# Adding the bias of the gates on TensorE and taking tanh straight from PSUM, in a two-block transformer kernel

## The reference, cut to what matters

```
mod = silu(c) @ w_ada + b_ada
u = modulate(rmsnorm(h, norm_mix_g), sh1, sc1)
z = u @ w_in
...
ga, gb = split(sigmoid(u @ w_gate + b_gate), 2)
h = h + g1 * ((ga * y_ret + gb * y_dsa) @ w_o)
```

## Time and profile before

| what | us |
|---|---|
| median of 3 runs (lowest, highest) | 908.58 (907.78, 908.63) |
| the profiled execution | 907.57 |
| its span in the trace | 905.9 |
| PE busy in the span | 891.5 |
| DVE, ACT, POOL busy | 680.6, 548.2, 209.8 |

### The profile page before, as it was taken

How to read it: one execution, slowest core, us unless ns; L and a number is a source line. 1 busy time by engine, 2 the same in 40 slices (tenths; PEclk the granted TensorE clock), 3 DMA queues, 4 the chain that set the end, 5 groups by cost and what they waited for, 6 DMA issues and landing times.

```text
span 905.9 us, 12878 instructions
## 1 busy us (share of the span) xinstructions
PE 891.5 (98%) x4423; PEld 733.7 (81%) x4423; DVE 680.6 (75%) x961; ACT 548.2 (61%) x885; POOL 209.8 (23%) x218
## 2 busy tenths in 40 slices
PE   8999999999999999999999999999999999999996
PEld 6888877888887888888867889778788888888885
DVE  5867688765767578778686544699899897968984
ACT  6656776788557443443485446754775585656763
POOL 4696037545312011111005500014300000000001
PEclk9999999999999999999999999999999999999998
DMA  8656756666865899999646657634374098969941
GB/s 283 189 172 205 223 160 197 222 190 229 275 190 181 308 296 314 320 304 312 209 126 202 188 155 241 208 102 155 117 250 152 6 344 302 321 238 337 377 166 47
DMA packets 124007, 199.59 MB, mean 220 GB/s; under 512 B 9601, under 2 KB 73793, under 8 KB 123697
## 3 DMA queue, kind: packets, MB, share of 16 engines
q1 hardware_dynamic: 118048, 177.17, 59.6%
q0 software_dynamic: 5904, 21.71, 7.4%
HBM read 197.79 MB, written 2.62 MB: 221 GB/s over the span
## 4 chain that ended last, share of the span: by engine, by line
PE 86%; DVE 8%; issue 2%; DMA 1%; ACT 1%; POOL 1%; SPq 0%; ACTq 0%; DVEq 0%; POOLq 0%
PE lin L2926 21%; PE lin L2928 20%; PE lin L2927 20%; PE turn L3145 3%; PE sco L2928 2%; PE sco L2927 2%; PE sco L2926 2%; DVE w_lo L1913 2%; PE lin L3038 1%; PE lin L3039 1%; PE lin L3029 1%; DMA raw<-in_w_in_dram 1%; PE turn L3193 1%; PE sco L3266 1%; PE lin L3707 1%
## 5 line engine op out<-in xcount | busy, mean ns | idle before, releaser
L1913 DVE TENSOR_TENSOR w_lo<-raw,w_hi 128x1024 fp32r<-128x1024 f32 x220 | 288.3, 1323 | 104.6 <-ACT w_hi L1163 102.0
L1163 ACT ACTIVATE w_hi<-raw 128x1024 fp32r<-128x1024 f32 x220 | 229.1, 1059 | 104.5 <-PE lin L2928 84.0
L2926 PE MATMUL lin<-w_hi,a_hi 128*128 128x512 f32 (+2 forms) x600 | 237.2, 395 | 0.7 <-DVE w_lo L1913 0.5
L2928 PE MATMUL lin<-w_hi,a_lo 128*128 128x512 f32 (+2 forms) x600 | 230.6, 384 | 0.0
L2927 PE MATMUL lin<-w_lo,a_hi 128*128 128x512 f32 (+2 forms) x584 | 224.0, 384 | 0.0
L2926 PEld LDWEIGHTS lin<-w_hi,a_hi 128*128 128x128 f32 x600 | 112.8, 188 | 27.4 <-issue 4.5
L2928 PEld LDWEIGHTS lin<-w_hi,a_lo 128*128 128x128 f32 x600 | 112.8, 188 | 23.1
L2927 PEld LDWEIGHTS lin<-w_lo,a_hi 128*128 128x128 f32 x584 | 110.0, 188 | 19.9
L1127 POOL TENSOR_TENSOR arena<-x,rows 128x256 f32<-128x256 f32 x3 | 2.2, 744 | 195.3 <-DVE x L2904 195.3
L1069 POOL DMA_DIRECT2D arena<-in_w_ada_dram x32 | 17.0, 530 | 122.0 <-DVE mod L2016 121.5
L1041 POOL TENSOR_TENSOR mod<-mod,rows 128x1024 f32<-128x1024 f32 x16 | 38.1, 2382 | 24.9 <-ACT rows L1456 24.5
(11 more groups left out here) (572 smaller groups left out, 1886.3 us busy)
## 6 DMA issues: line engine op xcount, KB each, us to landing
raw<-in_w_in_dram SPq DMA_DIRECT2D x76, 512.0 KB, 4.1
arena<-in_w_ada_dram POOLq DMA_DIRECT2D x32, 512.0 KB, 5.6
raw<-in_w_ffn_gate_dram SPq DMA_DIRECT2D x22, 512.0 KB, 5.2
raw<-in_w_ffn_up_dram SPq DMA_DIRECT2D x22, 512.0 KB, 5.8
raw<-in_w_ffn_down_dram SPq DMA_DIRECT2D x22, 512.0 KB, 4.3
rows<-in_w_ada_dram SPq DMA_DIRECT2D x16, 512.0 KB, 4.2
raw<-in_w_o_dram SPq DMA_DIRECT2D x16, 512.0 KB, 4.7
raw<-in_w_gate_dram SPq DMA_DIRECT2D x16, 512.0 KB, 4.6
```

Of the source, the lines that this page charges most:

```text
L1163: act.activation(w_hi[:, s, :], raw[:, s, :], ACT.Copy).then_inc(hi_ready, 1)
L1913: dve.tensor_tensor(w_lo[:, s, :], raw[:, s, :], w_hi[:, s, :].bitcast(F32), ALU.subtract)\
L2926: pe.matmul(dst, l_hi, r_hi, start=start, stop=False)
L2928: return pe.matmul(dst, l_lo, r_hi, start=False, stop=stop)
```

## The change

The bias goes to PE. ACT rounds the bias (all 2048 columns on all partitions) into a high part `bias_hi`, in the space of `gate2`. DVE makes `bias_parts`, in place of the bias: partition 1 gets (high part minus bias), and all other partitions get minus the bias, rounded. DVE also makes a column `minus_r` that is -1 on partitions 0 and 1 and 0 elsewhere. PE begins each gate block with one product of this column, repeated over 128 columns, and 512 columns of `bias_parts`, for each half of the tokens; it leaves high part plus low part of the bias in the bank, and the products of the block add to that. The first of them waits for `bias_split`. ACT takes tanh from PSUM with the evacuation, two instructions of 128 by 512 for a block, one unit after the block ends. At the start, the gains are loaded and transposed first, and the second run of idle products has six in place of eight.

```
-    order += [(f"gt{n}", DK, "dve") for n in range(4)]
+    order += [(f"gt{n}", DK, "act") for n in range(4)]
...
+        minus_r = sb("minus_r", [P, 1], F32R)
...
+        bias_raw = rows[:, 2:4, :].rearrange("p a n -> p (a n)")
+        bias_parts = rows_r[:, 2:4, :].rearrange("p a n -> p (a n)")
...
+        bias_hi = arena_r[:, bt2:bt2 + 2 * D]
...
             sp.dma_start(cst[:, 0:P], consts[:, 0:P]).then_inc(ident_in, 16)
-            sp.dma_start(x[:, 0, :], ins["x"][0, 0:P, :]).then_inc(x_in[0], 16)
             sp.dma_start(rows[0:DK, 0, 0:P], ins["ln_mix_pre"].rearrange("a (k p) -> (a k) p", p=P))\
               .then_inc(rows_in[0], 16)
+            sp.dma_start(x[:, 0, :], ins["x"][0, 0:P, :]).then_inc(x_in[0], 16)
...
-            sp.wait_ge(evac["dve"], BLOCKS["gt3"][4])
+            sp.wait_ge(evac["act"], BLOCKS["gt3"][4])
...                                                         (ACT, fill)
-                        if BLOCKS[name][1] + BLOCKS[name][2] == unit_at[0]:
-                            if BLOCKS[name][3] == "act":
-                                evacuate(name)
-                        if name in ("gt0", "gt1", "gt2") and sum(BLOCKS[name][1:3]) + 2 == unit_at[0]:
-                            gate_tanh(name)
+                        late = 1 if name[:2] == "gt" else 0
+                        if BLOCKS[name][1] + BLOCKS[name][2] + late == unit_at[0] and BLOCKS[name][3] == "act":
+                            evacuate(name)
...                                                         (ACT, evacuate)
+                    if kind == "gt":
+                        i = act.activation(gate2[:, t, n * W:(n + 1) * W], lin[:, bank + t, :], ACT.Tanh, scale=0.5)
...                                                         (ACT, before fill(0, "jn7"))
+            act.wait_ge(rows_in[2], 48)
+            act.activation(bias_hi, bias_raw, ACT.Copy).then_inc(bias_high, 1)
             fill(0, "jn7")
...                                                         (ACT, DSA)
-                if i == 4:
-                    gate_tanh("gt3")
...                                                         (DVE, evacuate)
-                if kind == "gt":
-                    dve.wait_ge(rows_in[2], 48)
-                    bias = rows[:, 2 + n // 2, (n % 2) * W:(n % 2) * W + W]
-                    for t in range(NT):
-                        i = dve.tensor_tensor(gate2[:, t, c], lin[:, bank + t, :], bias, ALU.add)
-                    i.then_inc(done, 1)
...
-                        dve.wait_ge(tanh_ready, NT + 4)
+                        dve.wait_ge(evac["act"], BLOCKS["gt3"][4])
...                                                         (DVE, after fill(0, "jn7"))
+            dve.wait_ge(bias_high, 1)
+            dve.scalar_tensor_tensor(out=minus_r[:, :], in0=ident[:, 0:1], scalar=-1.0, in1=ident[:, 1:2],
+                                     op0=ALU.mult, op1=ALU.subtract)
+            dve.scalar_tensor_tensor(out=bias_parts, in0=bias_hi.bitcast(F32), scalar=ident[:, 1:2], in1=bias_raw, op0=ALU.mult, op1=ALU.subtract).then_inc(bias_split, 1)
             fill(1)
...                                                         (DVE, DSA)
-                if i == 3:
-                    evacuate("gt3")
...                                                         (PE, product_unit)
+                    if start and name[:2] == "gt":
+                        pe.wait_ge(bias_split, 1)
+                        n, start = int(name[2:]), False
+                        for t in tokens:
+                            pe.matmul(lin[:, 2 * (number % 2) + t, :], minus_r[:, :].broadcast_to([P, P]),
+                                      bias_parts[:, n * W:(n + 1) * W], start=True, stop=False)
...                                                         (PE, start)
             pe.wait_ge(ident_in, 16)
+            pe.wait_ge(rows_in[0], 16)
+            pe.transpose(sco[:, 0, 0:DK], rows[0:DK, 0, 0:P], ident[0:DK, 0:DK]).then_inc(gain_turned, 1)
             keep_clock(4)
             pe.wait_ge(x_in[0], 16)
             turn_all("x1.0", [col(x[:, 0, :], k) for k in range(4)])
-            pe.wait_ge(rows_in[0], 16)
-            pe.transpose(sco[:, 0, 0:DK], rows[0:DK, 0, 0:P], ident[0:DK, 0:DK]).then_inc(gain_turned, 1)
             turn_all("x1.1", [col(x[:, 0, :], k) for k in range(4, 8)])
-            keep_clock(8)
+            keep_clock(6)
```

More of the change, by code:

```diff
@@ L585, in two_blocks @@
         shift_out = sem("shift_and_scale_copied")
+        bias_high = sem("gates_bias_high_part_ready")
+        bias_split = sem("gates_bias_parts_ready")
         early_summed = sem("early_rows_summed")
@@ L1227, in evacuate @@
                 for t in range(NT):
-                    if kind == "in" and n >= 8:
+                    if kind == "gt":
+                        i = act.activation(gate2[:, t, n * W:(n + 1) * W], lin[:, bank + t, :], ACT.Tanh, scale=0.5)
+                    elif kind == "in" and n >= 8:
                         c = (n - 8) * W
@@ L1245, in evacuate @@
                 i.then_inc(evac["act"], 1)
[L1247 to L1252, removed]
             def block_loop(first, pairs, target, scale=lambda t: 1.0, start=None):
@@ L1945, in evacuate @@
                 done = evac["dve"]
-                if kind == "gt":
-                    dve.wait_ge(rows_in[2], 48)
-                    bias = rows[:, 2 + n // 2, (n % 2) * W:(n % 2) * W + W]
-                    for t in range(NT):
-                        i = dve.tensor_tensor(gate2[:, t, c], lin[:, bank + t, :], bias, ALU.add)
-                    i.then_inc(done, 1)
-                elif kind in ("pa", "ro"):
+                if kind in ("pa", "ro"):
                     gate = gate1 if kind == "pa" else gate2
                     if kind == "ro":
-                        dve.wait_ge(tanh_ready, NT + 4)
+                        dve.wait_ge(evac["act"], BLOCKS["gt3"][4])
                     for t in range(NT):
```

## The result

The changed kernel takes 915.28 us (median of 6 runs, 914.97 to 915.56) against 908.16 (6 runs, 907.51 to 908.63): a ratio of 1.0078, with an interval of 1.0066 to 1.0090. It is 7.1 us slower. The forecast was 914.6 with a range of 913.2 to 917.2. The profiled execution took 915.27 us with a span of 913.6, 7.7 above that of before.

A forecast was written before the change was run, and what follows sets the result against it. The prediction took PE, busy 891.5 of 905.9 us, to bound the kernel. It summed 4.65 + 1.84 - 0.59 + 0.1 = +6.0 us onto the median 908.58, giving 914.6 us, range 913.2 to 917.2.

The forecast's parts named there:

- low clock: PE behind the stall: the sum kept the high clock, or took its loss as under 1 us.
- sparse stage: Last two additions, for gt3, taken from DVE: PE has 0.1 us left to win there, left at nothing.
- rival A: PE's idle time in the stall drops its clock, costing 1 to 2.1 us more; 916.2 us, chance 0.36.
- stall: PE's first gate product waits for `bias_split` behind in-order work on ACT and DVE: 4.65 us, between 4.2 and 5.1.
- eight products: Bias products added on PE in the four gate blocks, 0.23 us each: +1.84 us.
- end of retention: PE's wait before the transposes at 635.70 goes, as DVE's chain shortens or PE comes later: -0.59 us.
- start: Gains loaded first, two idle products fewer on PE: +0.1 us, between -0.3 and +0.6.
- half of the slow stretch at the start: Upper price of a clock fall: 4.1 us at slow pace, as at the kernel's start, loses 2.1 us.
- two-pass bound: Eight broadcast products on PE priced like the float32 one, two passes and 0.95 us each: 7.6 us.
- two reasons: Before 635.70: DVE's chain 2.5 us shorter, or PE 1.4 us later by six products; either exceeds 0.59.
- B: Bias parts ready before PE's first gate product at 569.95, so no stall: +1.35 us, 909.9 us, chance 0.04.
- C: DVE sets the beat from 570 to 635, PE's hidden waits swallow the stall: -3.6 us, 905.0 us, chance 0.03.

The follow-up runs named there:

- e1: The changed kernel with ACT's rounding of the bias and DVE's making of the parts moved earlier, to idle places; 908.31 us, ratio 1.0003 to the kernel before.
- e5: The changed kernel with 18 idle products of 128 by 128 on PE just before its wait for the parts; 912.83 us, ratio 1.0053 to the kernel before.
- e2: The changed kernel without the eight bias products and PE's wait, the bias left out of the gates; 906.36 us, ratio 0.9983 to the kernel before.
- e7: e1 with two additions of 128 by 512 given back to DVE in the sparse stage, results unread; 909.02 us, ratio 1.0012 to the kernel before.
- e3: The kernel before with only the start's edits (gains loaded and transposed first, six idle products in place of eight); 907.63 us, ratio 0.9993.
- e8: The kernel before with the change for gt3 alone, its 512 columns of bias split early, the old start kept; 907.67 us, ratio 0.9992.
- e9: e8 with the edits of the start added; 906.83 us against 908.05 for the kernel before, ratio 0.9987.
- e10_few_idle_products: The changed kernel with 8 idle products of 128 by 128 on PE before its wait for the parts; 912.86 us, ratio 1.0055 to the kernel before.

## Why the prediction was right

The direction, the place and the largest term were right, and the total was 1.1 us too low (+6.0 forecast, +7.1 measured), as two terms that it had left out of the sum, the low clock and the sparse stage, go opposite ways. That the sum came as near as it did is in part luck: one omission of 2.0 us was offset by one of 0.8, and the median of three runs that it was added to, 908.58, was 0.4 above that of six. The measured time lies between the forecast and rival A's 916.2, and it was A's mechanism that happened. Point by point, from starts on PE in the two traces (the column makes 7.6, the spans differ by 7.7):

| term | forecast | trace | by experiment |
|---|---|---|---|
| stall | 4.65 | 4.68 | 7.0 with the clock (e1) |
| low clock | 0 (rival A: 1 to 2.1) | 2.0 | 2.4 (e5) |
| eight products | 1.84 | 1.84 | 1.95 (e1 less e2) |
| end of retention | -0.59 | -0.5 | |
| sparse stage | 0 | -0.8 | 0.7 (e7 less e1) |
| start | +0.1 | +0.4 (spread of executions) | -0.5, not clear of 0 (e3) |

**The stall.** PE came 0.40 us later to the transposes before it (570.00 against 569.60), so the stall is 575.03 - 569.95 - 0.40 = 4.68 us. Each link came as worked out: the rounding lasted 1.94 for 1.92, the split started 1.80 later for 1.81, the low part 1.12 behind it, `minus_r` took 0.07 of the path, the parts 2.35 for 2.29. The step that mattered was to ask where in the two programs the new instructions stand: between instructions that PE's next product needs anyway, in series. The bias itself had landed long before.

**The clock.** Here the prediction chose wrong. Rival A happened, in all six runs; it had a chance of 0.36 and no place in the sum. The evidence in hand, a fall 2.7 us after the last product against an idle time of 4.4 us, spoke for it, and was discounted because it was one instance. In the stall the fall came about 1.9 us after the last product. Its price was within the bounds: from the first bias product to the first index score PE took 5.40 us (575.03 to 580.43), and 3.38 in e1_parts_earlier (569.88 to 573.26), so 2.0 us. The forecast's bound, half of the slow stretch at the start, gave 2.1. (Its "eight idle products" at 2.85 are four: each float32 product stands in the rows as two. The halved pace is read rightly.) By the Trainium skill's page "TensorE: Matmul & The Clock Gate" (section "Why this matters for your kernels"), a gap of idle time between bursts of products costs the high clock. The changed kernel's windows agree: 0.50 from 573 to 579 us.

**The products.** No rival price: the broadcast fp32r column costs what any product of this width costs. The pair of gt1 starts at 593.37 and the stage behind it is 0.46 us later, 0.23 a product. The two-pass bound of 7.6 us is excluded.

**The end of the retention stage.** The idle time before the transposes is gone. From the first sparse scores to the first transposes of probabilities PE takes 11.11 us in the kernel before (628.09 to 639.20) and in e3_start_alone, and 10.57 to 10.62 in the nine other kernels: 0.51 for 0.59. The prediction said that either of its two reasons would do, and the wait is gone with either: in e2 DVE has lost its additions and PE is not later; in e8 and e9 DVE keeps six of the eight additions, and PE is later by the 0.46 us of two bias products.

**The sparse stage.** This term was mis-sized: "PE has 0.1 us left to win, which I leave at nothing"; it was 0.8. The 0.1 came from idle time. The waits there are hidden under the modelled ends of products, and only the distances between starts show them. The Trainium skill's page "Trainium Kernel Development and Optimization" (section "Performance Expectations") says of a related question, how close a kernel is to roofline, that busy time of products is a bad metric for it and the busy share of weight loads a good one. The two windows above show the same for hidden waits: nearly the same busy time of weight loads (23.87 and 23.94 us) in 30.39 and 29.59 us, where PE's own busy time filled both. For the retention stage the even beat was the right reading, and there the distances were checked; in the sparse stage they were not.

**The start.** The trace of the changed kernel is 0.4 us later at the transposes of `dt4` (570.00 for 569.60), but eight other traces with the same start reach them between 569.35 (e2) and 569.76 (e5), and e8, which has the old start, at 569.97. So 0.4 us is within what two executions differ by, and not shown to be the change. ACT's first high part started at 6.26 for 6.35, within the 0.3 forecast.

**Rivals B and C.** B asked for parts that are ready in time. The places allowed it only by another order of the program, which e1_parts_earlier then gave: 908.31, where B had said 909.9. Of the 1.6 us between them, 0.4 is the median that B was counted from and 0.8 the sparse stage; the other 0.4 is about what the start gains by its medians, which no trace shows. C is excluded: with DVE's work taken away and nothing put on PE, e2 gained 1.5 to 1.8 us, not 3.6, and the retention outputs still begin 4.44 us apart (605.21 and 609.65 in the changed kernel).

## What to carry to other kernels

Before a new wait is put in front of a full engine, write down what stands ahead of its releaser on each engine of the chain, and where those engines are idle: the same three instructions cost 7 us in one place and nothing 6 us earlier. Count an idle gap of TensorE such as the 4.4 us here twice, for itself and for the products at half pace behind it, and try idle products in it, which gave back 2.4 us. When an engine is full, a saving on another engine is worth something only where distances between starts exceed their usual pace; find these places and pay there alone.

## What the runs showed of the hardware

The granted clock fell about 1.9 us after the last product in the stall of the changed kernel (the product ended at 570.60, and a mean of 0.76 over the microsecond from 572 puts the fall at about 572.5) and 2.7 us after it at the end of the span of the kernel before. An idle time of 2.56 us left it up in the profiled run of e10_few_idle_products. So the length of the gap alone does not decide.

From PE's return at 575.03 the clock took some 4.3 us to come back. The prediction read 4.1 us of slow pace at the start of the kernel before, but that time is not fixed either. In the profiled run of the changed kernel PE began at 2.95, and its six idle products after 6.80 still ran at the slow pace:

```profile
6.80 2.71 PE L3217 MATMUL sco<-cst 128*128 128x128 f32 x12
```

These are twelve records in 2.71 us, where the kernel before has sixteen in 1.95 from 6.88 on the earlier trace rows. So the slow pace lasted about 6 us there.
